# First attention of a two-block transformer kernel: seven heads' scores and all values from single FP32 products to three rounded passes

## The reference, cut to what matters

```python
logits = jnp.einsum('bqhd,bqkd->bqhk', qb, c_sel).astype(jnp.float32) * ATTN_SCALE
p = jax.nn.softmax(jnp.where(valid, logits, -jnp.inf), axis=-1).astype(c.dtype)
return jnp.einsum('bqhk,bqkd->bqhd', p, c_sel)
```

## Time and profile before

| | |
|---|---|
| median of three runs | 2030.82 us |
| the profiled execution's own time | 2030.99 us |
| its span | 2029.2 us |
| granted PE clock | 1.000 of full |
| PE busy | 2013.0 us (99%) |
| DVE busy | 892.7 us (44%) |
| ACT busy | 715.3 us (35%) |
| POOL busy | 1019.4 us (50%) |
| stage of the first attention | 311.8 to 412.7 us |

### The profile page before, as it was taken

One profiled execution on the slowest core, in us unless ns is written; L12 is line 12 of the kernel. 1 busy time (PEld: TensorE's weight loads), 2 busy tenths in 40 slices (PEclk: granted clock), 3 DMA queues, 4 the chain that ended last, 5 costly groups with the idle time before them and its releaser, 6 DMA issues.

```text
span 2029.2 us, 26701 instructions
## 1 busy us (share of the span) xinstructions
PE 2013.0 (99%) x9561; PEld 1675.0 (83%) x9561; DVE 892.7 (44%) x1401; ACT 715.3 (35%) x991; POOL 1019.4 (50%) x785
## 2 busy tenths in 40 slices
PE   8999999999999999999999999999999999999999
PEld 7898887778888888888888887889888888888887
DVE  7687755634333322153334113468865533332124
ACT  5412224434323223232222223566544423222232
POOL 5454442244555554455555444666654555554443
PEclk9999999999999999999999999999999999999999
DMA  5223232113333322333333232332322333333232
GB/s 173 89 84 95 93 104 63 42 62 104 104 84 102 103 94 78 110 92 103 94 92 99 93 98 84 89 103 70 90 88 83 98 89 103 100 86 99 94 109 83
DMA packets 254249, 188.80 MB, mean 93 GB/s; under 512 B 7584, under 2 KB 249760, under 8 KB 254144
## 3 DMA queue, kind: packets, MB, share of 16 engines
q1 hardware_dynamic: 253488, 187.53, 30.9%
q10 hardware_dynamic: 688, 0.31, 0.1%
HBM read 180.93 MB, written 2.10 MB: 90 GB/s over the span
## 4 chain that ended last, share of the span: by engine, by line
PE 96%; DVE 1%; POOL 1%; issue 1%; ACT 0%; DMA 0%; SPq 0%; ACTq 0%; POOLq 0%
PE ps L624 30%; PE ps L626 29%; PE ps L625 29%; PE ps L848 1%; PE ps L993 1%; PE ps L834 1%; PE ps L916 1%; PE ps L918 1%; PE ps L917 1%; PE ps L842 0%; PE ps L981 0%; PE ps L980 0%; PE ps L889 0%; POOL wlo L575 0%; DVE rest_of L1918 0%
## 5 line engine op out<-in xcount | busy, mean ns | idle before, releaser
L520 POOL TENSOR_TENSOR wlo<-raw,whi 128x512 fp32r<-128x512 f32 (+1 forms) x636 | 865.3, 1391 | 895.9 <-ACT whi L1057 878.4
L624 PE MATMUL ps<-xh,whi 128*128 128x512 f32 (+2 forms) x1912 | 732.7, 383 | 9.1 <-DVE xl L1468 7.6
L626 PE MATMUL ps<-xh,wlo 128*128 128x512 f32 (+2 forms) x1912 | 722.0, 378 | 0.0
L625 PE MATMUL ps<-xl,whi 128*128 128x512 f32 (+2 forms) x1912 | 721.9, 378 | 0.0
L1057 ACT ACTIVATE whi<-raw 128x2048 fp32r<-128x2048 f32 (+1 forms) x157 | 293.7, 1871 | 803.0 <-PE ps L626 800.1
L624 PEld LDWEIGHTS ps<-xh,whi 128*128 128x128 f32 (+1 forms) x1912 | 358.2, 187 | 78.0 <-issue 10.0
L626 PEld LDWEIGHTS ps<-xh,wlo 128*128 128x128 f32 (+1 forms) x1912 | 357.8, 187 | 68.0
L625 PEld LDWEIGHTS ps<-xl,whi 128*128 128x128 f32 (+1 forms) x1912 | 358.5, 187 | 64.9 <-issue 2.5
L1522 DVE TENSOR_TENSOR tmp<-ps,rs 128x512 f32<-128x512 f32 x148 | 102.1, 691 | 318.2 <-PE ps L626 298.9
L624 PE MATMUL ps<-fh,whi 128*128 128x512 f32 x528 | 205.4, 389 | 0.0
L625 PE MATMUL ps<-fl,whi 128*128 128x512 f32 x528 | 205.4, 389 | 0.0
(11 more groups left out here) (293 smaller groups left out, 2198.1 us busy)
## 6 DMA issues: line engine op xcount, KB each, us to landing
raw<-in_w_in SPq DMA_DIRECT2D x90, 512.0 KB, 4.6
raw<-in_w_gate_up SPq DMA_DIRECT2D x44, 512.0 KB, 4.7
raw<-in_ffn_w_gate SPq DMA_DIRECT2D x44, 512.0 KB, 4.0
raw<-in_ffn_w_up SPq DMA_DIRECT2D x44, 512.0 KB, 5.2
raw<-in_ffn_w_down SPq DMA_DIRECT2D x32, 512.0 KB, 4.0
raw<-in_w_down SPq DMA_DIRECT2D x16, 512.0 KB, 3.9
raw<-in_ffn_w_down SPq DMA_DIRECT2D x16, 384.0 KB, 3.3
raw<-in_w_b SPq DMA_DIRECT2D x8, 512.0 KB, 4.3
```

Of the source, the lines that this page charges most:

```text
L520: ins = pool.tensor_tensor(wlo[:, c % 2, cs], raw[:, c % 2, cs], whi[:, c % 2, cs].bitcast(F32), ALU.subtract)
L624: pe.matmul(o, w_of(whi), xhi, start=first, stop=False)
L625: pe.matmul(o, w_of(whi), xlo, start=False, stop=False)
L626: return pe.matmul(o, w_of(wlo), xhi, start=False, stop=last)
```

## The change

- Scores of heads 1 to 7 at q = 1, 2 and 3 are computed from a high and a low part: `qh` by `cTh`, `qh` by `cTl`, and the low query (put into `ath`) by `cTh`, three F32R matmuls for each product. The 528 columns of q = 3 become two products of 264. Head 0, and q = 0 of every head, stay as they are.
- All value products become three F32R matmuls: `ctok` by `pT`, `ctokl` by `pT`, `ctok` by `pTlo`; the 16-latent product likewise, with `ctoke` and `pTe`.
- ACT gets one copy of the latents (`cTh`, 528 columns) at the end of the conv stage and seven copies of 384 query columns (`query_high`), the first ahead of the attention and the others in steps 0 to 5.
- DVE gets the low latents by row (`cTl`) and by token (`ctokl`, `ctoke`), seven low queries (`query_low`), for each step the low part of the turned probabilities (`dsa_low`, behind ACT's copy), a second instruction for the corner in `dsa_edge_in` behind the first, and three more clearings of 16 columns or fewer ahead of the stage.
- PE waits for `pt_low` in each step 1 to 32, where before it waited for ACT's copy; for `ctok_split` in place of `ctok_done`; for `ct_split` once; for `q_split` in the scores.

```diff
-        ctok = at("ctok", 528, [P, QB + 1, P])
+        ctok = at("ctok", 528, [P, QB + 1, P], F32R)
+        ctokl = nc.alloc_sbuf_tensor_at("ctokl", [P, QB, P], F32R, offset=sq_start)
+        ctoke = nc.alloc_sbuf_tensor_at("ctoke", [META, P], F32R, offset=ssum_start)
+        cTh = at("cTh", 24896, [P, TM], F32R)
+        cTl = nc.alloc_sbuf_tensor_at("cTl", [P, TM], F32R, offset=rt_start)
...
-        pT = at("pT", 11520, [P, QB + 1, T])
+        qh = at("qh", 7424, [P, HEADS, T], F32R)
+        pT = at("pT", 11520, [P, QB + 1, T], F32R)
+        pTlo = at("pTlo", 25472, [P, QB, T], F32R)
+        pTe = at("pTe", 27520, [META, META], F32R)
+        edge = at("edge", 15328, [META, 2, META])
...
+        def split_scores(n):
+
+            return n >= QB and n % QB > 0
+
+        def score_parts(n):
+
+            w = META + P * (n % QB + 1)
+            first = w if w <= 512 else HALF if split_scores(n) else 512
+            return [slice(0, first)] + ([slice(first, w)] if first < w else [])
...
-            pe.wait_ge(ctok_done, 2)
+            pe.wait_ge(ctok_split, 1)
...
                             pe.wait_ge(A["pt_copy_d"], n)
+                            pe.wait_ge(pt_low, n)
...
+                pe.wait_ge(q_split, h)
+                for z, cs in enumerate(score_parts(n)):
+                    o = ps[:, b + z, 0:cs.stop - cs.start]
+                    pe.matmul(o, qh[:, h, qs_], cTh[:, cs], start=True, stop=False)
+                    pe.matmul(o, qh[:, h, qs_], cTl[:, cs], start=False, stop=False)
+                    mm = pe.matmul(o, ath[:, h, qs_], cTh[:, cs], start=False, stop=True)
...
-                first = seen_from(q)
-                mm = pe.matmul(o[:, first:T], ctok[:, q, :], pT[:, q, first:T], start=q == 0, stop=False)
-                if q == QB - 1:
-                    mm = pe.matmul(o[:, seen_from(QB):T], ctok[0:META, QB, :], pT[0:META, QB, seen_from(QB):T], start=False, stop=True)
+                first, last = seen_from(q), q == QB - 1
+                for k, w, x in ((0, ctok, pT), (1, ctokl, pT), (2, ctok, pTlo)):
+                    mm = pe.matmul(o[:, first:T], w[:, q, :], x[:, q, first:T], start=q == 0 and k == 0, stop=False)
+                if last:
+                    e = o[:, seen_from(QB):T]
+                    pe.matmul(e, ctok[0:META, QB, :], pT[0:META, QB, seen_from(QB):T], start=False, stop=False)
+                    pe.matmul(e, ctoke[:], pT[0:META, QB, seen_from(QB):T], start=False, stop=False)
+                    mm = pe.matmul(e, ctok[0:META, QB, :], pTe[:], start=False, stop=True)
...
+            pe.wait_ge(ct_split, 1)
...
+            act.wait_ge(c_done, 1)
+            act.activation(cTh[:], cT[:], ACT.Copy).then_inc(ct_hi, 1)
...
+            def query_high(h):
+
+                act.activation(qh[:, h, P:T], qT[:, h, P:T], ACT.Copy).then_inc(q_hi, 1)
+
+            query_high(1)
...
                         copy_turned(A, n, 5, pT, 1)
+                    if n + 2 < HEADS:
+                        query_high(n + 2)
...
+                    if (j, t) == (0, 0):
+                        dve.wait_ge(ctok_done, 2)
+                        dve.tensor_tensor(ctokl[:].rearrange("p q d -> p (q d)"), ps[:, 5, :],
+                                          ctok[:, 0:QB, :].rearrange("p q d -> p (q d)").bitcast(F32), ALU.subtract)
+                        dve.tensor_tensor(ctoke[:], ps[0:META, 7, 0:P], ctok[0:META, QB, :].bitcast(F32),
+                                          ALU.subtract).then_inc(ctok_split, 1)
...
+            dve.wait_ge(ct_hi, 1)
+            dve.tensor_tensor(cTl[:], cT[:], cTh[:].bitcast(F32), ALU.subtract).then_inc(ct_split, 1)
...
-                dve.tensor_copy(pT[0:META, q + 1, c:c + META], edge[:, n % 2, :]).then_inc(edge_in, 1)
+                hi = pT[0:META, q + 1, c:c + META]
+                link(dve.tensor_copy(hi, edge[:, n % 2, :]))
+                dve.tensor_tensor(pTe[:] if q == QB - 1 else pTlo[0:META, q + 1, c:c + META], edge[:, n % 2, :], hi.bitcast(F32),
+                                  ALU.subtract).then_inc(edge_in, 1)
+
+            def dsa_low(n):
+
+                h, q = divmod(n, QB)
+                dve.wait_ge(A["pt_copy_a"], n + 1)
+                block = slice(P * q, P * q + P)
+                dve.tensor_tensor(pTlo[:, 0:q + 1, block], ps[:, 5, 0:P * (q + 1)].rearrange("p (j t) -> p j t", j=q + 1),
+                                  pT[:, 0:q + 1, block].bitcast(F32), ALU.subtract).then_inc(pt_low, 1)
+
+            def query_low(h):
+
+                dve.wait_ge(q_hi, h)
+                dve.tensor_tensor(ath[:, h, P:T], qT[:, h, P:T], qh[:, h, P:T].bitcast(F32), ALU.subtract).then_inc(q_split, 1)
...
                     dsa_edge(n)
+                    dsa_low(n)
+                if n + 2 < HEADS:
+                    query_low(n + 2)
```

More of the change, by code:

```diff
@@ L136, in build @@
         rs = sb("rs", [P, TM])
+        rt_start = (nc.sbuf_base + 31) // 32 * 32
         rt = sb("rt", [P, TM])
+        sq_start = (nc.sbuf_base + 31) // 32 * 32
         sq = sb("sq", [P, TM])
@@ L239, in build @@
         sk2 = [at("sk20", 26624, [P, T], F32R), nc.alloc_sbuf_tensor_at("sk21", [P, T], F32R, offset=ssum_start)]
-        edge = rt[0:META, 0:2 * META].rearrange("p (z m) -> p z m", z=2)
         ysum, yhalf = rt[:, 0:T], sq[:, 0:T]
@@ L272, in build @@
         sc_zero = sem("sc_zero")
-        edge_in = sem("edge_in")
+        edge_in, pt_low = sem("edge_in"), sem("pt_low")
+        ct_hi, ct_split, ctok_split, q_hi, q_split = sem("ct_hi"), sem("ct_split"), sem("ctok_split"), sem("q_hi"), sem("q_split")
         ks_dup, qst_dup = sem("ks_dup"), sem("qst_dup")
@@ L831, in dsa_scores @@
                 h, q = divmod(n, QB)
[L832 to L836, removed]
+                b, qs_ = 1 + 2 * (n % 2), slice(P * q, P * q + P)
+                if not split_scores(n):
+                    for z, cs in enumerate(score_parts(n)):
+                        mm = pe.matmul(ps[:, b + z, 0:cs.stop - cs.start], qT[:, h, qs_], cT[:, cs], start=True, stop=True)
+                    return mm
+                pe.wait_ge(q_split, h)
+                for z, cs in enumerate(score_parts(n)):
+                    o = ps[:, b + z, 0:cs.stop - cs.start]
+                    pe.matmul(o, qh[:, h, qs_], cTh[:, cs], start=True, stop=False)
+                    pe.matmul(o, qh[:, h, qs_], cTl[:, cs], start=False, stop=False)
+                    mm = pe.matmul(o, ath[:, h, qs_], cTh[:, cs], start=False, stop=True)
                 return mm
@@ L1756, in dsa_unit @@
                 w, b = META + P * (n % QB + 1), 1 + 2 * (n % 2)
+                halves = lambda x: x
                 logits = ps[:, b:b + 2, :].rearrange("p b k -> p (b k)")[:, 0:w]
+                if split_scores(n) and w > 512:
+                    halves = lambda x: x.rearrange("p (z k) -> p z k", z=2)
+                    logits = ps[:, b:b + 2, 0:HALF]
                 dve.wait_ge(A["lg_ready"], n + 1)
@@ L1760, in dsa_unit @@
                     dve.wait_ge(A["exp_done"], n - 1)
-                dve.tensor_tensor_reduce(lm[:, n % 2, 0:w], logits, sc[:, n % QB, 0:w], -1.0, 3.0e38, ALU.add, ALU.min,
+                dve.tensor_tensor_reduce(halves(lm[:, n % 2, 0:w]), logits, halves(sc[:, n % QB, 0:w]), -1.0, 3.0e38, ALU.add, ALU.min,
                                          nmx[:, n:n + 1]).then_inc(A["mx_done"], 1)
@@ L1777, in dsa_edge_in @@
                 c = seen_from(q + 1)
-                dve.tensor_copy(pT[0:META, q + 1, c:c + META], edge[:, n % 2, :]).then_inc(edge_in, 1)
-            for j in range(1, QB):
-                link(dve.memset(pT[:, j, seen_from(j):P * j], 0.0))
+                hi = pT[0:META, q + 1, c:c + META]
[11 more added lines that the diff above has]
+                dve.tensor_tensor(ath[:, h, P:T], qT[:, h, P:T], qh[:, h, P:T].bitcast(F32), ALU.subtract).then_inc(q_split, 1)
+            for x in (pT, pTlo):
+                for j in range(1, QB):
+                    link(dve.memset(x[:, j, seen_from(j):P * j].bitcast(F32), 0.0))
             for n in range(2):
@@ L1784, in _ @@
                 normalise(A, n, pr[:, n % 2, 0:META + P * (n % QB + 1)])
+            query_low(1)
             for slot in range(4 * 2 * DK):
```

## The result

The changed kernel takes 2039.0 us (median; 2038.7 to 2040.1), the kernel before 2031.1 us beside it: 7.9 us slower, ratio 1.0038, 95% interval 1.0027 to 1.0048. Forecast were 2036.1 us and a range of 2029.5 to 2040.5. The profiled execution of after is 2040.1 us, 2038.3 of it span. From the first scores to the first matmul of the next stage, before took 100.82 us (311.84 to 412.66) and after takes 108.91 (312.78 to 421.69): all of the loss lies in the stage of the first attention.

A forecast was written before the change was run, and what follows sets the result against it. The prediction took PE to bound the kernel (96% of the chain): 5.7 us saved against 11.0 us of new waits for DVE's low part gave +5.3 and 2036.1 us, range 2029.5 to 2040.5.

The forecast's parts named there:

- PE's saving, 5.7: First attention on PE: three F32R passes for F32 products save 3.3 us in scores, 2.4 in values; bounds 5.2 and 6.5.
- the last value piece: 144 columns and 16 latents on PE become six thin F32R matmuls: 0.75 us taken, between 0.66 and 0.81.
- The plain part of the new wait, 5.6: PE's value piece waits for ACT's copy, then `dsa_low`: 0.8 us at q = 1, 1.9 at q = 2, 2.9 at q = 3.
- The 0.15 at each of steps 12, 24 and 28: PE's wait for the low part at q = 3 where two slots lie between: 0.15 us each.
- step 31, forecast at 0.34 to 0.38: PE's wait for a q = 2 low part with one slot, 1.50 us of path against 0.78 + 0.38 of cover.
- DVE and POOL on top, 7.2: Extra PE waits: about 5 us from corner instructions held in three POOL windows, 1.8 in the first head; bounds 2 and 9.
- Step 8: PE waits 1.7 to 2.0 us because DVE's second corner instruction waits out a whole POOL block ahead of `dsa_low`.
- Step 7's stop: PE's q = 2 wait of 0.34 to 0.38 us, and 0.4 more from DVE's late work in the first head.
- the first head: POOL until 319, three more clearings and six low queries make DVE late: waits 0.85, 1.2, 0.75 us, 1.8 us added.
- The deductions, 1.2 for over-walking and 0.6 for stalls that swallow each other: Taken off PE's summed waits: the walk of the kernel before overstated waits by 1.2 us; overlapping stalls brought 11.6 to 11.0.
- Signs: Expected in the changed profile: PE idle 11 to 12 us in the stage, ended by `pTlo`; F32R distances; long corner subtractions.
- the rival with DVE as the bound: `dsa_low` also delays reciprocal and scaling, so transposes wait; DVE passes 25 of 25 us: 2042 us, chance 0.10.

The follow-up runs named there:

- e6_spread: Against the changed kernel, the query splitting of heads 2 to 7 runs one head at a time at steps 2, 6, 10 and so on; 2038.5 us, ratio 1.0035.

## Why the prediction was right

Sign and mechanism held. Its terms, against what came out:

- **PE's saving, 5.7:** 5.2. The mis-sized term is the last value piece, 0.81 where 0.75 was taken; the upper of the two ends given was the right one.
- **The plain part of the new wait, 5.6:** with POOL away, the stops are where they were forecast, most with the size: 0.57 shown at steps 16 and 20, 0.82 with the 0.25 that the bracket hides (forecast 0.84), and 0.43 at 32, 0.68 with it (0.7). Two entries were wrong. The 0.15 at each of steps 12, 24 and 28 appears in no run. And step 31, forecast at 0.34 to 0.38, shows 0.69, 0.94 with what is hidden: I covered it with 0.38 of scores, but step 31 issues none, since there is no step 33. In the changed kernel's profile step 20 has no stop shown.
- **DVE and POOL on top, 7.2:** POOL's blocks are worth 6.4 us. The subtraction waits out a whole block or nearly so, as forecast (1.22, 1.15, 1.21 us), and steps 18 and 19 stop for 0.86 and 1.25. Step 8 stops for 0.96, 1.2 with what is hidden, where 1.7 to 2.0 was forecast. Step 7's stop is the queries', as I had it (0.97 with POOL away, 0.29 with them spread), but it is 1.2 with what is hidden, where the list had 0.35 and 0.4. In the first head the sizes were right (0.85, 1.2, 0.75 forecast for steps 1 to 3; 0.95, 1.12, 0.67 with 0.25 added to what is shown), but part of the reason was not: spreading the queries' parts changed nothing there. Step 1 stops because POOL holds the scaling of the probabilities, 1.30 us where it takes 0.36 without POOL's blocks, and the low part is queued behind it; the stop is gone in both kernels with these blocks cut, and 0.33 without the low part. The kernel before has the same hold (1.32 us, shown in the last section), and the prediction read only the corner's copies. Step 2's stop stays with POOL away (0.77), with the queries spread (0.91) and without the low part (0.88, ended by the corner's copy); it was there before (0.64), and what makes DVE late at that step stays open. That this head has no value piece to put beside the path may be part of it; no run shows that.
- **The deductions, 1.2 for over-walking and 0.6 for stalls that swallow each other:** these failed. The waits are 13.1 us (7.9 + 5.2), where the list summed to 12.8 before deductions and 11.0 after. That the 12.8 comes so near is partly luck: steps 8, 12, 20, 24 and 28 had too much in it, steps 7 and 31 too little. Of the missing 2.9 us the waits are 2.1, the last value piece is 0.5, and 0.3 is the kernel before itself, 2031.1 us beside this run and 2030.8 when I predicted.
- **Signs:** 9.65 us shown instead of 11 to 12, because the bracket leaves out 0.25 a stop, which I hadn't seen. `pTlo` ended them, transposes did not wait for `pr`, and DVE was at 19.43 of 25 us, not 21.3: the rival with DVE as the bound stayed out, and the wait moved behind the value piece showed it.

On the rule cited ahead, that VectorE and GpSimd lock each other out of a shared port pair (the Trainium skill, "SBUF — State Buffer", section "SBUF: two separate sides"), the trace agrees: 1.22 us for a subtraction with two SBUF inputs, 0.16 for the same with one in PSUM. On the other, the floor of about 25 ns between starts (the Trainium skill, "TensorE: Matmul & The Clock Gate", section "Wait — 56ns, not 53.3ns?"), the trace does not contradict the floor, but the estimate worked out from it fails: the three thin passes lie 0.07 and 0.11 us apart (360.55, 360.62, 360.73) and six of them cost 0.81, not about 0.3.

## What to carry to other kernels

When a pass is split in parts, price the chain that makes the low part before the matmuls: here 5.2 us of PE time was bought with 13 us of waits, and edits that only moved waits, operands and small copies gave back 10.2. Put a wait directly ahead of the first instruction that needs it, behind any work that doesn't; that alone was worth 7.0 us. A tiny VectorE instruction between SBUF tiles can cost a whole GpSimd block and hold up everything queued behind it, so give it a PSUM operand or another engine. And look in the trace of the kernel before for every instruction that GpSimd's blocks stretch, not only for the kind that the change adds.

## What the runs showed of the hardware that I had not expected

The scaling of the probabilities, `pr`, is held by POOL too. In the kernel without the low part one of 272 columns takes 1.19 us beside POOL's blocks, where the same shape takes 0.36 with these blocks cut (317.46, above). The kernel before shows it as well, beside the blocks of 314.03 to 319.06 and of 336.60 to 341.64:

```profile
339.68 1.19 DVE L1801 TENSOR_SCALAR pr<-pr,rden 128x272 f32<-128x272 f32 x1
```

```profile
317.90 1.32 DVE L1751 TENSOR_SCALAR pr<-pr,rden 128x272 f32<-128x272 f32 x1
338.23 1.05 DVE L1751 TENSOR_SCALAR pr<-pr,rden 128x272 f32<-128x272 f32 x1
```

In the profiled execution of the changed kernel PE's granted clock fell for some 3.4 us, behind the stops at steps 18 and 19: it is 0.50 of full from 375 to 378, and 400 columns of scores lie 0.33 us apart instead of 0.18: the lower of the two levels of 1.2 and 2.4 GHz. The stretch, in the changed kernel and in `e6_spread`, whose stops there are as long (0.85 and 1.23):

```profile
370.00:390.00 20.00, 18.55 (x98) 15.78 (x99) 14.99 (x53) 7.26 (x20) 3.13 (x3) 0.91 0.16 53
```

```profile
370.00:390.00 20.00, 17.48 (x100) 14.72 (x101) 16.52 (x57) 7.97 (x22) 3.73 (x3) 1.00 0.16 54
```

At half speed over 3.4 us it is worth up to 1.7 us in that one execution (behind it step 20's stop is missing, 0.58 in `e6_spread`), and the median lies 1.1 below it. It may also be part of the 0.8 us by which this execution's stage exceeds the sum of 7.3; no run shows that. With the same stops and no fall in the other kernel, what triggers it stays open.
